# Late inputs, first expert rows and first expert weights: where the SP and GpSimd queues send them in an encoder layer

## What is computed

```python
h = _rms_norm(x, norm1_w[i])
u = jnp.einsum('btd,dc->btc', h, w_in[i])
...
y_a = _rwkv7_mixer(u_r, ...)            # 8 heads x 64, both directions
y_b = _hgrn2_mixer(u, lb_all[:, i], hgrn_gnorm_w[i])   # 4 heads x 128, both directions, chunks of 32
x = x + jnp.einsum('btc,cd->btd', jnp.concatenate([y_a, y_b], axis=-1), w_out[i])
h2 = _rms_norm(x, norm2_w[i]).reshape(B * T, D)
x = x + _hier_moe(h2, ...)              # top-1 of 4 groups, then top-2 of 8 SwiGLU experts
...
eid = grp[:, None] * EXPERTS_PER_GROUP + top_i
...
xbuf = jnp.zeros((P, D), h.dtype).at[dest].set(h[tok_sorted])
def run_block(args):
    xb, e = args
    hid = jax.nn.silu(xb @ w_gate[e]) * (xb @ w_up[e])
    return hid @ w_down[e]
```

## Time and profile before

| | us |
|---|---|
| median of 3 runs | 2636.4 |
| lowest and highest run | 2632.0, 2639.8 |
| profiled execution | 2644.0 |
| its span | 2642.4 |
| TensorE busy in it | 2365.1 (90%) |
| VectorE, ScalarE, GpSimd busy | 990.0, 755.1, 233.1 |
| mixing stage ends, common stage begins | 1320.1 |
| common stage ends, routing block begins | 1794.9 |
| first product of the first expert block | 1838.5 |

### The profile page before, as it was taken

One profiled execution on the slowest core, in us unless ns is written; L12 is line 12 of the kernel. 1 busy time (PEld: TensorE's weight loads), 2 busy tenths in 40 slices (PEclk: granted clock), 3 DMA queues, 4 the chain that ended last, 5 costly groups with the idle time before them and its releaser, 6 DMA issues. The chain is left out here.

```text
span 2642.4 us, 64852 instructions
## 1 busy us (share of the span) xinstructions
PE 2365.1 (90%) x28302; PEld 1557.2 (59%) x28302; DVE 990.0 (37%) x2172; ACT 755.1 (29%) x1456; POOL 233.1 (9%) x322
## 2 busy tenths in 40 slices
PE   6989999879999999999748899993999999999980
PEld 4444444345555555565447666752888888888860
DVE  2236576533554645535537434432000000000007
ACT  4124454423544444434412112220111111111002
POOL 0001122100000000000011001002111111111110
PEclk8989999889999999999868899995999999999995
DMA  4103343433333343432285222116788888888838
GB/s 126 32 17 131 123 135 112 168 83 84 91 106 78 92 108 75 120 91 52 93 265 186 81 85 87 49 44 223 298 327 326 322 322 322 323 323 327 332 143 294
DMA packets 338329, 435.81 MB, mean 165 GB/s; under 512 B 162864, under 2 KB 268336, under 8 KB 329904
## 3 DMA queue, kind: packets, MB, share of 16 engines
q1 hardware_dynamic: 326528, 397.17, 44.8%
q0 software_dynamic: 11568, 35.20, 3.3%
HBM read 335.92 MB, written 96.36 MB: 164 GB/s over the span
## 5 line engine op out<-in xcount | busy, mean ns | idle before, releaser
L1098 PE MATMUL m_ps_pp<-hT,h_wcol 128*128 128x512 f32 x864 | 437.4, 624 | 26.5 <-DVE m_decay L1313 26.5
L504 PE MATMUL r_pp<-hT,r_wcol 128*128 128x512 f32 x720 | 313.1, 596 | 1.8 <-PEq L268 1.6
L2452 PEld LDWEIGHTS e_ps_g<-e_xT,e_wg 128*128 128x128 f32 x2048 | 236.6, 194 | 16.2 <-issue 16.2
L2452 PE MATMUL e_ps_g<-e_xT,e_wg 128*128 128x128 f32 x2048 | 236.9, 277 | 1.0 <-DVE e_xT L2491 1.0
L504 PEld LDWEIGHTS r_pp<-hT,r_wcol 128*128 128x128 f32 x720 | 137.1, 192 | 170.6 <-issue 170.0
L2462 PE MATMUL e_ps_y<-e_wd,e_hid 128*128 128x512 f32 x512 | 227.3, 597 | 9.5 <-DVE e_hid L2496 9.5
L2452 PE MATMUL e_ps_u<-e_xT,e_wu 128*128 128x128 f32 x2048 | 233.9, 275 | 0.0
L2452 PEld LDWEIGHTS e_ps_u<-e_xT,e_wu 128*128 128x128 f32 x2048 | 231.3, 192 | 0.0
L1098 PEld LDWEIGHTS m_ps_pp<-hT,h_wcol 128*128 128x128 f32 x864 | 144.9, 190 | 139.6 <-issue 99.8
L2496 DVE TENSOR_TENSOR e_hid<-e_ps_u,e_silu 128x512 f32<-128x512 f32 x32 | 22.1, 691 | 444.4 <-PE e_ps_u L2452 444.4
L1979 PE MATMUL o_ps_out<-o_wout,y 128*128 128x512 f32 x384 | 180.0, 614 | 5.1 <-DVE y L2188 5.1
(11 more groups left out here) (340 smaller groups left out, 3372.3 us busy)
## 6 DMA issues: line engine op xcount, KB each, us to landing
e_wg<-in_moe_w_gate_dram SPq DMA_DIRECT2D x32, 2048.0 KB, 7.8
e_wu<-in_moe_w_up_dram SPq DMA_DIRECT2D x32, 2048.0 KB
e_wd<-in_moe_w_down_dram SPq DMA_DIRECT2D x32, 2048.0 KB, 12.8
ar<-r_ar SPq DMA_DIRECT2D x24, 512.0 KB, 2.7
kb<-r_kb SPq DMA_DIRECT2D x24, 512.0 KB, 2.7
m_ar<-ar SPq DMA_DIRECT2D x48, 256.0 KB, 4.4
m_kb<-kb SPq DMA_DIRECT2D x48, 256.0 KB, 3.5
kq<-h_kqst SPq DMA_DIRECT2D x24, 512.0 KB, 4.1
```

Source lines behind the costliest of these rows:

```text
L504: last = nc.tensor.matmul(pp[s][:], wcol[q][:, c], self.hT[:, c, s * SPAN:(s + 1) * SPAN], start=c == 0, stop=c == KT - 1)
L1098: last = nc.tensor.matmul(pp[n % 2][:], wcol[k % 3][:, c], self.hT[:, c, span(s)], start=c == 0, stop=c == KT - 1)
L2452: last = nc.tensor.matmul(ps[:, q * P:(q + 1) * P], w[u][:, c, q * P:(q + 1) * P], xT[u][:, c * P:(c + 1) * P], start=c == 0, stop=c == KT ...
```

## The change

It moves the sending of data; no product, sum or table changes.

- **Mixing stage.** The columns (h, 4) of the output gates go to the end of `COLS`; so the last head's k and q are ready three steps sooner, and its stores fall inside the loop. `store_o` sends two DMAs (one for each direction) in place of eight.
- **Common stage, SP.** w_out goes out as eight pieces, one in each of `r_mean(0)` to `r_mean(7)`, behind the item's `load_y`. The empty slots go out in `r_mean(8)`, the norm and router weights in `r_mean(9)`, three tiles of x in `r_mean(10)`. `load_g(0)` comes ahead of the small scales.
- **Common stage, end.** For the last pair placed there, `weigh` comes behind the last `msq`, and `place` behind `turn(11, 0)`, that is on VectorE behind the last `h2n`.
- **Memory.** The scan's tiles (kq, v, qs, k3, pt, state, kt, k2) lie in the weight buffers of the first expert and in the second's gate buffer, so that the buffers `wg0`, `wu0`, `wd0`, `wg1` are kept through both stages. In the order below `e_wg<-kq` and `e_wu<-itok` are therefore loads of kq and v. The first expert's weights are loaded by `scanned()`, once the scan's last products are done.
- **Routing block.** GpSimd loads the first list, whose place is known, directly behind the last scatter, then lists 1 to 3 and gathers rows for blocks 0 and 1, all in this block. SP waits for the rows of block 0 and the plan, and then loads the second expert's weights, in this block.

```diff
-COLS = [(h, q) for h in range(PAIRS) for q in range(5) if q < 4 or h >= GATED]
+COLS = [(h, q) for h in range(PAIRS) for q in range(4)] + [(h, 4) for h in range(GATED, PAIRS)]
...
-                        for g in range(G):
-                            sp.dma_start(self.yT[g // PAIRS, g % PAIRS, :, (c - 3) * CH:(c + 1) * CH],
-                                         oacc[c // 4 % 2][:, g]).then_inc(out_stored, 16)
+                        for d in range(2):
+                            sp.dma_start(self.yT[d, 0:PAIRS, :, (c - 3) * CH:(c + 1) * CH].rearrange("j p t -> p j t"),
+                                         oacc[c // 4 % 2][:, d * PAIRS:(d + 1) * PAIRS]).then_inc(out_stored, 16)
...
-                    store_kq(2 * PAIRS - 1, 2)
-                    store_dc(2 * PAIRS - 1)
                     store_o(CHUNKS - 1)
...
-            kq = [sb(f"g_kq{u}", [P, 2, G, P]) for u in range(2)]
+            kq = [flat(self.wg[0])[:, 2 * D * u:2 * D * (u + 1)].rearrange("p (two g n) -> p two g n", two=2, g=G)
+                  for u in range(2)]
+            v = [four[1][u].rearrange("p (d n) -> p d n", d=2) for u in range(2)]
...
                     late("turn", n - 1, 1.1, 0)
+                    if n == TILES:
+                        route("place", n - 1)
...
+                    if n < TILES - 1:
+                        route("weigh", n)
                     late("turn", n - 1, 1.1, 1)
...
                     late("msq", n, 0)
-                    route("place", n)
+                    if n < TILES - 1:
+                        route("place", n)
+                    else:
+                        route("weigh", n)
...
+                    def scanned():
+
+                        self.waits(sp, bank_o.full(("o", TILES - 1, 1)), bank_k.done(("kv", TILES - 1, 1)))
+                        self.load_gate_up(sp, 0, 0)
+                        self.load_down(sp, 0, 0)
...
+                    def r_mean(k):
+                        load_y(k + RING_B)
+                        if k < KY:
+                            sp.dma_start(wout[:, k], a["w_out"][0, k * P:(k + 1) * P]).then_inc(wout_loaded, 16)
+                        elif k == KY:
+                            self.waits(sp, self.index.at("unused", 0))
...
+                        elif k == KY + 1:
...
+                        elif k == KY + 2:
+                            for n in range(RING_X):
+                                load_x(n)
...
                 def _(sp):
-                    self.load_gate_up(sp, 0, 0)
-                    self.load_down(sp, 0, 0)
+                    self.waits(sp, (self.e_x_loaded[0], 16), dve.at("expert", 0))
+                    second = sp.value_load(self.expert[0:1, 1:2], min_val=0, max_val=NE - 1)
+                    self.load_gate_up(sp, second, 1)
+                    self.load_down(sp, second, 1)
...
                     self.scatter(eng, G)
                     eng.wait_ge(self.scattered, 2 * TILES * 16)
+                    with nc.allow_non_contiguous_dma(reason="pairs of indices"):
+                        eng.dma_start(self.e_slots[:, 0:1], self.by_unit()[0:1].rearrange("o p k -> p o k")
+                                      ).then_inc(self.e_first_loaded, 16)
+                        self.waits(eng, dve.at("unit_i", 0))
+                        for b in range(1, 4):
+                            self.load_slots(eng, slice(b, b + 1))
+                        self.waits(eng, (self.e_first_loaded, 16))
+                        self.gather(eng, 0, 0, slice(0, 1))
+                        self.waits(eng, (self.e_slots_loaded, 48))
+                        self.gather(eng, 1, 1, slice(1, 2))
```

More of the change, by code:

```diff
@@ L1775, in schedule @@
                     gap(c, budget)
+                run("scanned")
                 gap(TILES, 1e9)
@@ L1884, in _ @@
                             sp.dma_start(dst, w).then_inc(scales_loaded, 16)
-                        for k in range(RING_G):
-                            load_g(k)
+                        load_g(1)
                         load_v(1)
-                        self.waits(sp, self.index.at("unused", 0))
-                        rows = self.slots.rearrange("(p k) o -> p k o", p=P)
-                        for q in range(NUNIT // P):
-                            sp.dma_start(rows[:, q * P:(q + 1) * P], self.unused[:]).then_inc(self.cleared, 16)
@@ L1902, in _ @@
+                    schedule(scores=scores, out=out, scanned=scanned, r_mean=r_mean, n_wide=lambda k: load_g(k + RING_G),
                              turn=lambda n, h: load_x(n + RING_X) if h else store_h2(n))
```

122 lines of the change are left out of this document (58 added, 64 removed).

## The result

The changed kernel takes 2610.4 us (median of 4 runs, 2605.1 to 2614.3) against 2638.1 for the kernel before in the same session: a ratio of 0.990, 95% interval 0.987 to 0.992, so 27.7 us less. Timed twice more, the ratio was 0.9885 (0.9851 to 0.9918) and 0.9877 (0.9848 to 0.9906), which is 30 and 33 us (the medians alone differ by 34.8 and 28.6). The prediction said 43.2 less, 2593.2. The direction holds, and the time lies 4.4 us above the forecast's own range, 2585 to 2606.

A forecast was written before the change was run, and what follows sets the result against it. TensorE fills the expert loop, so only its idle stretches elsewhere can shrink. 21.9 - 2.0 + 13.8 + 1.7 + 4.8 + 3.0 = 43.2 us off the median 2636.4 gives 2593.2 us, range 2585 to 2606.

The forecast's parts named there:

- Part 1: Start of common stage: item 2's loads go ahead of the late inputs; 21.9 us less, minus 2.0 for new waits between items.
- The 14 us more for eight pieces: w_out's transfers: a serial fixed cost per transfer would make eight pieces 14 us slower; left out of the sum.
- Part 2: Routing block to TensorE's first expert transposes: scatters, lists and rows come sooner without weights moving; 13.8 us less, bounds 10.6 and 16.5.
- the handover of 2.3 + 0.5: End of routing block: SP's three issues with register loads, 2.3 us, and the barrier, 0.5, precede TensorE's first transposes.
- Part 3: Last tile of the common stage: no table load before the last root and an earlier reciprocal; 1.7 us less to the last logits.
- The 3.1 by the Trainium skill: Last root on ScalarE: the last tile's term if each table load also cost 1.38 us of drain; not used in the sum.
- Part 4: Mixing stage: 4.8 us less from last output to the next stage's first issue, and 3.0 less inside the stage.
- The v waits: Inside the mixing stage: TensorE's 3.3 us in four places behind SP issue bursts; 3.0 us less, bounds 0 and 3.9.
- A: Common stage: the stall moves, with item 2 and followers landing at 15 us, not 5; 2603 us, chance 0.12.
- B: TensorE behind item 2's wait: the clock stays up, 10 us of slow work become 5; 2588 us, chance 0.13.
- C: Common stage items become bound by their transfers, so slower; priced at a 22 us landing, 2642 us, chance 0.02.
- D: SP's queue: an earlier wait holds it as long as the transfers did; only 16 us gained, 2620 us, chance 0.05.

## Why the prediction was wrong in size

**Base and sum.** I took differences from one trace off a median, which is right only for what does not vary. The three traces of the changed kernel and the two of the kernel before give 37.9 us less from the mixing stage on, and 34.6 with the start, where 43.2 was forecast. The timed ratios give 28 to 33. The stretch ahead of the mixing stage, which the change leaves alone, ended between 535.5 and 552.1 us in the 17 traces, and the clock moves another 10 us. Most of what is left between traces and medians is which executions were traced: those of the kernel before took 5.9 and 1.7 us more than their medians, those of the changed one 5.3 less, 1.0 and 1.5 more, on the mean 4.7 us of difference. Part of the 37.9 is luck as well: of the 3.4 us less from item 2 to the last logits the earlier root explains 2.2, and the 1.4 us less in the last two stages have no cause in the change.

**Part 1, late inputs: right.** 20.6 for 21.9. The landing was 5.0 us (forecast 5.2); SP had item 2's second load on its way 20.3 us behind the stage's first issue where the forecast, by 1339.3 - 1320.1, had 19.2, since the issue of y took 1.85 us. No wait was added between the items, where I had put 2.0; the loads had the room that the prediction worked out. The 14 us more for eight pieces, an estimate from the Trainium skill (DMA: Bandwidth & Descriptors, section Anatomy of one DMA), did not come. That section gives its fixed cost for transfers that GpSimd issues, and w_out goes out on SP. Here the single transfer of 4 MB landed in 15.4 us, the pieces of 0.5 MB in 5.7 each by their median, behind work that did not wait for them. (The 0.98 of the earlier trace rows, read there as transfers of 0.5 MB together, is until about 1354 mostly that single one, sent at 1338.65.)

**Part 2, the first expert: size right, one step wrong.** 12.8 for 13.8. First list, list loads and gather came as forecast: first list 14.5 us behind the block's start in both. The rows were in 4.3 us behind their gather, by SP's first issue that waits for them, not 3.4. The step that failed is the handover of 2.3 + 0.5, put on SP's issues; with these away nothing changed, and what held the block's end was POOL's second gather, which the prediction did not name. I had followed the wait of SP and not asked what else is in flight on the engines at a block's end. The first expert's weights at the end of the scan cost nothing that can be seen, as forecast: from item 2 to the last logits it is 419.9 us without them and 416.5 to 425.2 with them.

**Part 3, the last tile: mechanism right, cover lost.** The root gave 2.2 for 1.7: the reciprocal came 1.7 us sooner, as forecast, and the transposes behind it took 0.46 us less at the higher clock. (The 3.1 by the Trainium skill, ScalarE: Activation LUTs, section What ACT_TABLE_LOAD costs, did not come: no drain of 1.38 us is in those 1.7.) Placing moved later on POOL, though, and the block ended 1.6 us later for it, where I had said that the four scatters end "still ahead of the block's end", and put a bound of 0.7 on losing that cover. They did end ahead of the logits (1767.3 against 1768.2), but the end of the block comes 3 us behind them.

**Part 4, the mixing stage: tail exact, inside wrong, and this is the largest miss.** The tail gave 4.8 for 4.8. For the inside I forecast 3.0 less, with bounds 0 and 3.9, and it was 3.5 more: 6.5 us of the shortfall, without which the time would have come out near 2604, inside the range (an estimate: 2610.4 less 6.5). Two things failed. The v waits, 3.3 us in four places, were taken to go almost whole, and 2.0 us of them stayed, in three places. Without the stall the stage is 2.0 shorter on the mean (0.7 to 4.2 in the four traces), and with the old order and the two stores only 0.6. And "shortens nothing that I see on TensorE's chain" took a reorder as free because its arithmetic is the same. A reorder also changes the distance at which a ring of buffers is used again. The gate buffer's store was one step late in SP's queue all along; only the four columns between two gate columns had covered that. A bound for it could have been had from the order of the instructions: span 0 of the next gate column directly behind span 2 of the last.

**The rivals.** A (the stall moves to the items) is excluded by the 3.1 us wait and the run with the inputs back in one burst. B (the clock stays up) did not show in that place: in the first 5 us behind the wait the granted clock was 0.50 in the first traces of both kernels, and 2708 matmuls kept TensorE busy 392.4 us after and 392.6 before. It did show at the last tile, where the transposes behind the shorter wait still ran at 1.00. C and D did not come (D's 16 us should read 14.7: 7.8 from part 4 and half of 13.8). A new stall did arise, but in another stage, which no rival named. For the inside of the mixing stage the lower bound was 0, a gain that shrinks to nothing; a reorder can also lose.

## What to carry to other kernels

When work is reordered, list every ring of buffers that it uses and count the steps between two uses of the same buffer, before and after; then look where in the queue the store stands that frees it. At the end of a block ask which engine has a transfer of the software queue in flight, for in these runs the next block started behind it. And take a second trace of the kernel before when terms of a few us are added up: it shows which stage lengths are fixed to a fraction of a us and which are drawn.

## What the runs showed of the hardware

A block that ends with POOL's software transfers ends some time behind their issue: 3.0 us behind the last scatter (1767.31 to 1770.27; 2.6 to 3.6 in the nine traces that end the common stage so). TensorE's first transposes in the next block start 4.7 to 5.3 us behind the second of two gathers in eleven traces, and 4.2 and 4.3 behind a single one, where the rows themselves may be what they wait for. SP's issues ahead of the block's end made no difference to it (27.8 us with them, 27.9 without).

TensorE's granted clock differs between executions of one kernel: the same 2708 matmuls took 382.5 and 392.4 us at 0.93 and 0.91, and of 17 executions of the kernel before in one session those at 0.942 took 2621.7 and 2623.8 us, those at 0.934 2641.4 and 2644.4. The wait for a store of 5.7 us on ScalarE cost TensorE 2.8 us of idling and then some 5 us at 0.56 of the clock, an estimated 2.2 us more than at full clock, so the slow work behind that short wait cost about as much as the wait.
